# The stage of V in a hybrid decoder trunk: fetched rows summed in PSUM, low halves of the weight tiles made by GpSimd

## The reference

```python
q = einsum("bsd,de->bse", h, w_query)            # 8 heads, two halves
s1, s2 = scores of the halves against 128 sub-keys each
v1, i1 = top_k(s1, 16); v2, i2 = top_k(s2, 16)
top_v, top_i = top_k(v1 + v2 for all pairs, 16)
expert = e1 * 128 + e2                           # 8 x 16 = 128 experts for a token
gate = softmax(top_v)
act = gelu(einsum("td,thkd->thk", x, expert_u[expert])) * gate
y = einsum("thk,thkd->td", act, expert_v[expert])
```

## Time and profile before

| | |
|---|---|
| median of three runs | 3100.2 us (3099.47 to 3101.4) |
| the profiled execution's own time | 3100.26 us |
| its span, first to last instruction | 3098.5 us |
| PE busy | 3024.0 us, 98% |
| PE weight loads busy | 2701.9 us, 87% |
| DVE busy | 2709.6 us, 87% |
| ACT busy | 1495.0 us, 48% |
| POOL busy | 1680.2 us, 54% |
| chain that ended last | PE 80%, DVE 11%, ACT 3%, issue 2%, POOL 2%, DMA 2% |
| two stages of V, L1179, in that chain | 22% (banks) and 11% (gbank) |
| DMA | 273 GB/s over the span, 375 and 351 in the two stages of V |
| mean granted TensorE clock | 0.990 |

### The profile page before, as it was taken

The page is one execution under the profiler, slowest core; times in us unless marked ns, Lnnn a source line. Parts: engine busy times, 40 slices in busy tenths (PEclk is TensorE's granted clock), DMA queues, the critical chain, the costliest instruction groups (busy, mean ns, idle before and its releaser), DMA issues.

```text
span 3098.5 us, 45070 instructions
## 1 busy us (share of the span) xinstructions
PE 3024.0 (98%) x15648; PEld 2701.9 (87%) x15648; DVE 2709.6 (87%) x4904; ACT 1495.0 (48%) x2668; POOL 1680.2 (54%) x989
## 2 busy tenths in 40 slices
PE   7999999999999999999999899999999999999999
PEld 6888899999999888888777678999999998888887
DVE  7987997999999889998687769989999999888887
ACT  4344335766665333343444643346666663333332
POOL 3434356888896555542245433467988986422221
PEclk9999999999999999999899899999999999999999
DMA  6633246999999999999335342357999999999996
GB/s 258 241 103 123 82 150 214 317 336 356 323 343 368 382 386 393 382 392 375 111 110 175 84 134 82 106 183 259 362 334 337 346 342 378 381 373 368 350 350 234
DMA packets 320605, 846.16 MB, mean 273 GB/s; under 512 B 28208, under 2 KB 149056, under 8 KB 320400
## 3 DMA queue, kind: packets, MB, share of 16 engines
q1 hardware_dynamic: 189952, 437.83, 41.0%
q0 software_dynamic: 74000, 268.81, 23.6%
q10 hardware_dynamic: 56448, 136.86, 11.7%
HBM read 735.91 MB, written 94.90 MB: 268 GB/s over the span
## 4 chain that ended last, share of the span: by engine, by line
PE 80%; DVE 11%; ACT 3%; issue 2%; POOL 2%; DMA 2%; SPq 0%; ACTq 0%; DVEq 0%; POOLq 0%
PE banks L1179 22%; PE gbank L1179 11%; PE banks L1159 9%; PE banks L1161 9%; PE banks L1160 9%; PE banks L1139 4%; PE banks L1141 4%; PE banks L1140 4%; DVE u_rows L2151 3%; PE gbank L1531 2%; POOL w_lo L593 1%; DVE hot L2128 1%; PE gbank L1485 1%; PE banks L1251 1%; POOL u_rows L610 1%
## 5 line engine op out<-in xcount | busy, mean ns | idle before, releaser
L593 POOL TENSOR_TENSOR w_lo<-raw,w_hi 128x1024 fp32r<-128x1024 f32 x351 | 868.7, 2476 | 567.6 <-ACT w_hi L685 563.7
L685 ACT ACTIVATE w_hi<-raw 128x1024 fp32r<-128x1024 f32 x613 | 646.8, 1055 | 603.6 <-PE banks L1179 350.5
L618 POOL DMA_INDIRECT v_rows<-v_dram,row_of x256 | 376.6, 1471 | 598.6 <-DVE fetched L2166 585.1
L1159 PE MATMUL banks<-h_hi,w_hi 128*128 128x384 f32 x2048 | 686.6, 335 | 2.7 <-POOL w_lo L593 2.7
L1160 PE MATMUL banks<-h_lo,w_hi 128*128 128x384 f32 x2048 | 684.7, 334 | 0.0
L1161 PE MATMUL banks<-h_hi,w_lo 128*128 128x384 f32 x2048 | 684.5, 334 | 0.0
L2151 DVE CUSTOM_DVE_ANT_0 u_rows<-u_rows,h_rows 128x1024 f32<-128x1024 f32 x256 | 449.8, 1765 | 5.3 <-DMA u_rows<-u_dram,row_of 5.2
L610 POOL DMA_INDIRECT u_rows<-u_dram,row_of x256 | 359.7, 1405 | 135.3 <-DVE z L2151 97.0
L1159 PEld LDWEIGHTS banks<-h_hi,w_hi 128*128 128x128 f32 x2048 | 384.7, 188 | 4.4 <-POOL w_lo L593 4.4
L1160 PEld LDWEIGHTS banks<-h_lo,w_hi 128*128 128x128 f32 x2048 | 384.5, 188 | 0.0
L1161 PEld LDWEIGHTS banks<-h_hi,w_lo 128*128 128x128 f32 x2048 | 384.4, 188 | 0.0
(11 more groups left out here) (377 smaller groups left out, 5079.2 us busy)
## 6 DMA issues: line engine op xcount, KB each, us to landing
raw<-stream_dram SPq DMA_DIRECT2D x613, 512.0 KB, 6.3
gel_dram<-gel ACTq DMA_DIRECT2D x248, 192.0 KB, 5.0
gin<-gel_dram SPq DMA_DIRECT2D x62, 768.0 KB, 10.5
g_dram<-stage ACTq DMA_DIRECT2D x56, 768.0 KB, 11.0
gates<-g_dram SPq DMA_DIRECT2D x64, 672.0 KB, 7.4
ada_w<-ada_dram ACTq DMA_DIRECT2D x34, 512.0 KB, 6.3
ada_out<-ada_dram ACTq DMA_DIRECT2D x18, 512.0 KB, 4.8
ada_first<-ada_dram SPq DMA_DIRECT2D x8, 1024.0 KB, 17.6
```

What stands on the lines that cost most here:

```text
L593: pool.tensor_tensor(w_lo[:, s, :], raw[:, s, :], w_hi[:, s, :].bitcast(F32), ALU.subtract).then_inc(split_lo, 1)
L618: pool.indirect_dma_start(v_rows[:, j % V_ROWS, :], None, (v0, v1)[layer], bass.IndirectOffsetOnAxis(ap=row_of[:, j:j + 1], axis=0)).then_ ...
L685: act.activation(w_hi[:, s, :], raw[:, s, :], ACT.Copy).then_inc(split_hi, 1)
L1159: pe.matmul(out, wh, h_hi[:, k, 0:DENSE_T], start=(k == 0), stop=False)
```

## The change

In the stage of V the running sum of the fetched rows moves from SBUF (`fetched`) to the two free banks of `gbank[0]` (`fetched_sums`): the first step writes it there, the next 126 read it and write it there, and the last one reads it there and writes `fetched` in SBUF, where `turn_sums` reads it. VectorE no longer makes the low halves of V tiles 2 to 127. GpSimd makes them: the low of V tile j-1 right behind `v_fetch(j)` for j from 3 on, and that of tile 127 at the end. Before its first v fetch it waits until VectorE has made the lows up to V tile 1.

```diff
+    fetched_sums = gbank[0][:].rearrange("p t n e -> p (t n e)")
...
             pool.wait_ge(tile_done, DENSE[layer] + NKEYS)
+            pool.wait_ge(split_lo, DENSE[layer] + NKEYS + LOW_AHEAD)
             for j in range(PICKS):
                 v_fetch(layer, j)
+                if j >= V_ROWS - 1:
+                    low(DENSE[layer] + NKEYS + LOW_AHEAD + j - V_ROWS + 1)
                 dotted = dot_beside(j - V_ROWS)
                 if dotted is not None and dotted + U_ROWS - 1 < PICKS:
                     u_fetch(layer, dotted + U_ROWS - 1)
+            for v in range(LOW_AHEAD + PICKS - V_ROWS + 1, NKEYS):
+                low(DENSE[layer] + NKEYS + v)
...
                 if j == 0:
-                    add = dve.tensor_scalar(fetched[:], row, share[:, 0:1], None, ALU.mult)
+                    add = dve.tensor_scalar(fetched_sums, row, share[:, 0:1], None, ALU.mult)
                 else:
                     dve.wait_ge(S("added"), past["added"] + j)
-                    add = dve.scalar_tensor_tensor(out=fetched[:], in0=row, scalar=share[:, j:j + 1], in1=fetched[:],
-                                                   op0=ALU.mult, op1=ALU.add)
+                    add = dve.scalar_tensor_tensor(out=fetched[:] if j == PICKS - 1 else fetched_sums, in0=row,
+                                                   scalar=share[:, j:j + 1], in1=fetched_sums, op0=ALU.mult,
+                                                   op1=ALU.add)
...
             for v in range(NKEYS):
-                if v + LOW_AHEAD < NKEYS:
-                    low(DENSE[layer] + NKEYS + v + LOW_AHEAD)
                 if v + V_AHEAD < NKEYS:
                     product(v + V_AHEAD)
```

## The result

The changed kernel takes 3361.3 us (median of 4 runs, 3358.7 to 3362.5), the kernel before beside it 3099.8: a ratio of 1.084, interval 1.083 to 1.086, or 261 us more. The profiled execution took 3362.1 us, with a span of 3360.3. The prediction had the sign, slower, but 3250 us, and its range ended at 3330.

What follows compares the result with a forecast made beforehand. TensorE was taken to bound the V stages at 4.08 us a tile. Layer 0: 34 + 17 + 15 + 21 - 1.5 = 85.5; layer 1: 34 + 17 + 15 - 1.5 = 64.5; 3100.2 + 150 = 3250 us, range 3130 to 3330.

Steps and rivals of the forecast that it cites:

- low, chain, rest of the fetch, next low: V-stage cycle of GpSimd and VectorE (a_low, product), modelled on the U stage: 2.42 + 1.09 + 0.83 + 0.01 = 4.35 us.
- the term of 0.83: GpSimd in V: rest of a held fetch after VectorE's chain ends, 0.83 us of each cycle.
- 1.5 us of reserve per layer: Start of V: fetches waiting for earlier additions leave no reserve of lows; 1.5 us per layer given back.
- on no path in either case: VectorE's V additions, taken at 1.28 us, delay nothing; its tile stays under 2.6 us of 4.08.
- 126 x 0.27 = 34 us per layer: V stage: each of 126 tiles takes 0.27 us more than TensorE's tile, 34 us per layer.
- the extras: V stages: U dots 17 us and u fetches 15 us per layer, modulation dots 21 us in layer 0.
- GpSimd and VectorE have no spare time left: V stages: a cycle of 4.35 us cannot absorb the added dots and u fetches, so they cost time.
- A: Rival: in V the chain fits into gap and fetch, cycle 3.55 to 3.68, not slower, 3100 us; chance 0.13.
- B: Rival: in V only the added dots and u fetches cost, less absorbed reserves: 69 us, 3169; chance 0.20.
- C: Rival: in V the chain also holds the low, lows 4.75 apart, 3350, or 3300 mixed; 0.14 with D and E.
- D: Rival: gaps on TensorE lower its granted clock, adding to the forecast or C; 0.14 together with C and E.
- E: Rival: V additions with one SBUF operand still exclude the low, giving C's cycle; 0.14 together with C and D.

Runs made afterwards that it cites:

- e1: Changed kernel with the sums kept in PSUM but all V lows back on VectorE: 3098.8 us, ratio 0.9998 to the kernel before.
- e9: Changed kernel plus a memset of 128 unused columns on GpSimd between each v fetch and its low: 3184.8 us, ratio 1.029 to the kernel before.
- e3: Changed kernel with eight V row buffers instead of four, so a fetch no longer waits for the newest addition: 3242.8 us, ratio 1.046 to the kernel before.
- e5: Changed kernel with VectorE's second product left out, so 48 columns of the activations lack their gate: 3153.1 us (one run).
- e8: Changed kernel with each V low on GpSimd split into two instructions of 512 columns: 3388.1 us, ratio 1.093 to the kernel before.

## Why the prediction was wrong in its size

**Right.** The V stage before was bound by TensorE, so nothing was to be won (e1: 0.9998). Operations with two SBUF operands and GpSimd's lows exclude each other, one with an operand in PSUM runs beside a low (e9: 1.28). The addition costs 1.28 us in PSUM. (The 1.21 to 1.22 that I gave for an operation that reads PSUM at this width stands in none of the rows cited for it; the kernel before shows it at L2128, 1.22.) The loss comes from the order of VectorE and GpSimd, not from busy time, with TensorE waiting for the lows. The clock stayed (0.99 and 1.00 in the two stages). A dot of U costs 1.15.

**The step that failed** is "low, chain, rest of the fetch, next low", 4.35 us, taken over from the U stage. Three things in it were wrong.

First, the chain is not queued behind a low as a whole. a_low and the first product run during the fetch, and the fetch takes 1.01 us, not 1.76: the term of 0.83 doesn't exist here. Only the second product is held (behind a modulation dot the first one). The prediction saw two states, chain before the low (harmless) and chain behind the low. It missed the cut through the chain. The row that would have told it stands in the U stage of the kernel before, where I had read other rows. VectorE, and GpSimd beside it:

```profile
515.95 4.09 DVE L2151 CUSTOM_DVE_ANT_0 u_rows<-u_rows,h_rows 128x1024 f32<-128x1024 f32 x1
```

```profile
515.55 0.96 POOL L610 DMA_INDIRECT u_rows<-u_dram,row_of  x1
516.53 2.42 POOL L593 TENSOR_TENSOR w_lo<-raw,w_hi 128x1024 fp32r<-128x1024 f32 x1
```

A dot of 1.22 us starts 0.40 after a fetch, 0.58 before the low, and ends 1.09 after the low: it did none of its work in that time. Nor was the fetch of 2.69 us the rule in the V stages before: the median of the 128 fetches is 1.01 us in layer 0 and 0.94 in layer 1.

Second, I summed durations where a loop had to be closed. I named the wait, "v_fetch(j), which waits for addition j-4", and priced it at 1.5 us of reserve per layer. But with all four buffers full, addition j-4 is the newest one, and it stands on VectorE behind the held product. So the additions, which I put "on no path in either case", are on the path: 1.20 + 0.27 + 1.02 + 0.02 + 2.39 + 0.07. e3 takes this wait away: 119 us back. e5 and e9 take the hold of the product away: 208 and 176. The hold and the wait are both needed for the 4.97. The term 126 x 0.27 = 34 us per layer should have been 128 x 0.89 = 114.

Third, the extras. The 12 u fetches, put at 15 us per layer, cost nothing: GpSimd idles 1.55 us in each cycle. "GpSimd and VectorE have no spare time left" held for VectorE alone. The modulation dots cost half of the 1.15 I gave each.

**The rivals.** A: wrong for the change, but e9 shows that its order exists. B and C are out with the 4.35. C's 3300 to 3350 is nearest in size, by another mechanism: no low was held by the chain. D: no. E: the addition was not stretched. The V times of 607 and 587 us that I forecast are, by chance, those of e3 (604.6 and 585.6).

**The rule of the Trainium skill**, "SBUF — State Buffer", section "Who interferes with whom", that tensor_tensor does not stall descriptor generation: in the changed kernel a fetch with a_low and a product beside it takes 1.01 us, close to the rule, while the earlier trace rows show 2.69. I used the row for a stage with other work on VectorE: both fetches start beside an a_low, but in the earlier trace rows VectorE's own low of 1.22 us follows it, and in the changed kernel the two products follow. That the long operation makes the difference is not tested. What followed from the rule, rival A, came true no more than mine, since neither looked at the second product. The same section says that the engine which loses the shared port is fully blocked, not slowed down; the 0.20 us product that takes 2.97 agrees, though by the records the product had been asked for first.

## What to carry to other kernels

Before moving an operation to a half-idle engine, write the waits down as a closed loop, with each buffer's release at its newest value, and sum once around it: that sum, not an engine's busy time, is the tile's time. A short operation in a chain that shares a port with a long one on another engine can cost the long one's whole duration, and it matters which operation of the chain falls on the boundary: 0.15 us of shift decided between 0.20 and 2.97 us here (e9). An operand in PSUM frees an operation only if that operation's turn comes while the other engine holds the port.

## What was not expected of the hardware

- A wide low on GpSimd holds a VectorE operation with two SBUF operands whose turn comes about half a microsecond before the low's recorded start: 2.97 us instead of 0.20 (low of 2.39), 2.43 with a low of 1.85, but 0.22 with one of 16 columns. In the kernel before, the dots of U whose turn came up to 0.50 ahead of a low right behind a fetch were held (7 of 7), those from 0.60 on were free (19 of 19). In the changed kernel 228 second products at 0.41 to 0.45 were held. In e9, with a memset directly ahead of the low, the border lies at 0.52 to 0.58.
- This reach ahead is missing where the low comes out of a wait. In e3 the low starts after 0.55 us of waiting for ScalarE; an a_low with its turn 0.40 before it takes its own 0.54 (194 of them at 0.50 or less took 0.54 or 0.55). The first product, which starts beside that low, takes its own 0.49, and it is the low that grows, from 2.39 to 2.75. What the port does in that half microsecond stays open.
- GpSimd can keep the port between two operations in a row (e8: 3.10 us through both halves), but VectorE does get in when its turn comes while the first is already running (e8, 1.58 us). Between two operations of VectorE GpSimd gets in: in e3 a low does between the two products, and the second waits 2.40 us.
- 0.22 us of added work a tile on GpSimd made the changed kernel 176 us faster (e9).
